# Which engine makes the low parts of the second MLP's down products: one of seven on VectorE, or four of seven

## What is computed

```python
        h2 = rmsnorm(x, mlp_norm_w[l])
        u = jax.nn.relu(jnp.einsum('bld,df->blf', h2, w_up[l]))
        x = x + jnp.einsum('blf,fd->bld', u * u, w_down[l])

    return rmsnorm(x, final_norm_w)
```

## Time and profile before

| | us |
|---|---|
| median of 3 runs | 1609.27 |
| lowest to highest | 1608.09 to 1610.73 |
| the profiled execution, by the same clock | 1609.46 |
| its span in the trace | 1607.6 |
| TensorE busy | 1563.9 (97% of the span) |
| VectorE busy | 916.2 (57%) |
| GpSimd busy | 790.2 (49%) |
| ScalarE busy | 531.6 (33%) |

### The profile page before, as it was taken

The page is one execution under the profiler, slowest core; times in us unless marked ns, Lnnn a source line. Parts: engine busy times, 40 slices in busy tenths (PEclk is TensorE's granted clock), DMA queues, the critical chain, the costliest instruction groups (busy, mean ns, idle before and its releaser), DMA issues.

```text
span 1607.6 us, 19248 instructions
## 1 busy us (share of the span) xinstructions
PE 1563.9 (97%) x7495; PEld 1286.0 (80%) x7495; DVE 916.2 (57%) x1185; ACT 531.6 (33%) x760; POOL 790.2 (49%) x289
## 2 busy tenths in 40 slices
PE   9999999999999999999999999999999998989886
PEld 7887788888888888888888887877789886868764
DVE  5902588900246666666006489987555156382798
ACT  3012121200135443443124244257433334242334
POOL 5874288677760445445440003421251448556476
PEclk9999999999999999999999999999999999999998
DMA  6232032233242332332232232221232503214021
GB/s 223 90 120 79 1 112 92 92 105 105 79 131 80 105 105 79 104 104 89 95 118 73 89 97 79 81 52 26 80 131 79 183 27 127 83 56 154 0 79 53
DMA packets 127382, 147.00 MB, mean 91 GB/s; under 512 B 5143, under 2 KB 98375, under 8 KB 127304
## 3 DMA queue, kind: packets, MB, share of 16 engines
q1 hardware_dynamic: 125430, 141.05, 27.9%
q10 hardware_dynamic: 1874, 4.85, 0.9%
HBM read 143.79 MB, written 2.10 MB: 91 GB/s over the span
## 4 chain that ended last, share of the span: by engine, by line
PE 85%; POOL 5%; DVE 4%; issue 3%; ACT 2%; DMA 1%; POOLq 0%; DVEq 0%; SPq 0%; ACTq 0%
PE ps L812 26%; PE ps L814 25%; PE ps L813 25%; PE ps L967 3%; PE ps L1042 2%; POOL w_lo L795 1%; POOL w_lo L797 1%; PE ps L1209 1%; POOL w_lo L759 1%; PE ps L1030 1%; POOL tail_lo L795 1%; PE ps L1226 1%; DVE a_lo L2290 1%; POOL w_hi L754 1%; DVE x L2237 1%
## 5 line engine op out<-in xcount | busy, mean ns | idle before, releaser
L759 POOL TENSOR_TENSOR w_lo<-raw,w_hi 128x1024 fp32r<-128x1024 f32 x166 | 420.5, 2554 | 496.4 <-ACT w_hi L1312 493.6
L812 PE MATMUL ps<-hT_hi,w_hi 128*128 128x512 f32 (+1 forms) x848 | 324.5, 383 | 0.8 <-POOL w_lo L759 0.5
L813 PE MATMUL ps<-hT_lo,w_hi 128*128 128x512 f32 (+1 forms) x848 | 323.2, 381 | 0.0
L814 PE MATMUL ps<-hT_hi,w_lo 128*128 128x512 f32 (+1 forms) x848 | 323.2, 381 | 0.0
L754 POOL TENSOR_TENSOR w_hi<-raw,cells 128x2048 fp32r<-128x2048 f32 x35 | 129.5, 3701 | 126.5 <-PE ps L812 125.3
L812 PEld LDWEIGHTS ps<-hT_hi,w_hi 128*128 128x128 f32 x848 | 159.4, 188 | 33.9 <-issue 2.3
L814 PEld LDWEIGHTS ps<-hT_hi,w_lo 128*128 128x128 f32 x848 | 159.4, 188 | 30.6
L813 PEld LDWEIGHTS ps<-hT_lo,w_hi 128*128 128x128 f32 x848 | 159.4, 188 | 30.4
L1312 ACT ACTIVATE w_hi<-raw 128x2048 fp32r<-128x2048 f32 (+1 forms) x58 | 109.6, 1890 | 128.3 <-PE ps L812 106.5
L812 PE MATMUL ps<-w_hi,hT_hi 128*128 128x512 f32 (+2 forms) x400 | 151.6, 379 | 0.0
L813 PE MATMUL ps<-w_lo,hT_hi 128*128 128x512 f32 (+2 forms) x400 | 150.1, 375 | 0.0
(11 more groups left out here) (368 smaller groups left out, 3161.7 us busy)
## 6 DMA issues: line engine op xcount, KB each, us to landing
raw<-in_w_in SPq DMA_DIRECT2D x86, 512.0 KB, 4.7
raw<-in_w_up SPq DMA_DIRECT2D x60, 512.0 KB, 4.8
raw<-in_w_down SPq DMA_DIRECT2D x34, 512.0 KB, 4.2
raw_tail<-in_w_down SPq DMA_DIRECT2D x20, 512.0 KB, 4.7
raw<-in_w_out SPq DMA_DIRECT2D x16, 512.0 KB, 4.2
raw_tail<-in_w_up SPq DMA_DIRECT2D x16, 512.0 KB, 4.9
raw<-in_w_ret_o SPq DMA_DIRECT2D x8, 512.0 KB, 4.0
raw<-in_w_sgu_o SPq DMA_DIRECT2D x8, 512.0 KB, 4.0
```

The costliest lines, as they stand in the source:

```text
L759: nc.gpsimd.tensor_tensor(lo[:, c], raw[:, s, c], hi[:, c].bitcast(f32), ALU.subtract).then_inc(unit_split, 1)
L812: first = nc.tensor.matmul(dst, a_hi, b_hi, start=start, stop=False, skip_group_check=onto)
L813: nc.tensor.matmul(dst, a_hi, b_lo, start=False, stop=False, skip_group_check=onto)
L814: return first, nc.tensor.matmul(dst, a_lo, b_hi, start=False, stop=stop, skip_group_check=onto)
```

## The change

Products 3, 5 and 6 of each set get their weights' low part from VectorE too, beside product 2; products 0, 1 and 4 and all ups stay with GpSimd. VectorE makes it right behind the `a_lo` of the same step. On ScalarE `a_hi` of a step now goes ahead of `hi` of the same step. TensorE's list and SyncE's list stay as they are. `AT` is only another name for the places in `STREAM`, and the rewritten conditions of the sums give the same sums in the same steps.

```diff
-VECTOR_LOW = 2
+VECTOR_LOW = (2, 3, 5, 6)
...
-    by_vector = [kind == "down" and n == VECTOR_LOW for kind, _, n in STREAM]
+    by_vector = [kind == "down" and n in VECTOR_LOW for kind, _, n in STREAM]
...
                 if at_v + 2 < N:
-                    tail_high(at_v + 2)
                     if STREAM[at_v + 2][0] == "down":
                         token_high(at_v + 2)
+                    tail_high(at_v + 2)
                 square(at_v, 0)
...
+                nearest = STREAM[at_v + 1]
+                if nearest[0] == "down" and 2 <= nearest[2] <= 4:
+                    weight_sum(nearest[1], ADDS[nearest[2] - 1])
                 if at_v + 2 < N and STREAM[at_v + 2][0] == "down":
                     token_low(at_v + 2)
+                    if low_count(at_v + 2)[0]:
+                        weight_low(at_v + 2)
...
-                if kind == "down" and n == 0:
-                    weight_low(at_v + 2)
                 take(at_v, 0)
```

More of the change, by code:

```diff
@@ L246 @@
 STREAM = second_mlp()
-START = [STREAM.index(("down", q, 0)) for q in range(FF2_Q)]
+AT = {step: v for v, step in enumerate(STREAM)}
 RAW_SLOTS, W_SLOTS, A_SLOTS = 5, 3, 3
 def low_count(v):
-    by_vector = [kind == "down" and n == VECTOR_LOW for kind, _, n in STREAM]
+    by_vector = [kind == "down" and n in VECTOR_LOW for kind, _, n in STREAM]
     return by_vector[v], by_vector[:v + 1].count(by_vector[v])
@@ L1675, in token_high @@
                 if a_n >= A_SLOTS:
-                    before = START[(a_n - A_SLOTS) // 7] + (a_n - A_SLOTS) % 7
+                    before = AT["down", (a_n - A_SLOTS) // 7, (a_n - A_SLOTS) % 7]
                     act.wait_ge(tail_started, before + 2)
@@ L2247, in weight_sum @@
                     await_loaded(dve, "down", q, "B12")
-                    await_low(dve, START[q])
+                    await_low(dve, AT["down", q, 0])
                     made = V.tensor_tensor(out, raw_part(q, "B12"), out, ALU.subtract)
@@ L2251, in weight_sum @@
                     await_loaded(dve, "down", q, "B22")
-                    await_low(dve, START[q] + 2)
+                    await_low(dve, AT["down", q, 2])
                     made = V.tensor_tensor(out, raw_part(q, "B22"), out, ALU.subtract)
@@ L2258, in weight_sum @@
                 else:
-                    await_low(dve, START[q] + 1)
+                    await_low(dve, AT["down", q, 1])
                     dve.wait_ge(weights_added, 4 * q + 2)
@@ L2303, in _ @@
                 kind, q, n = STREAM[at_v]
-                coming = next((c for c in range(FF2_Q) if START[c] - at_v in (1, 2)), None)
-                if kind == "down" and n == 0:
[L2306 to L2310, removed]
+                coming = next((c for c in range(FF2_Q) if AT["down", c, 0] - at_v in (1, 2)), None)
+                if kind == "down" and n < 2:
+                    token_sum(q, TOKEN_SUMS[2 + n])
                 if coming is not None:
-                    token_sum(coming, TOKEN_SUMS[2 - (START[coming] - at_v)])
+                    token_sum(coming, TOKEN_SUMS[2 - (AT["down", coming, 0] - at_v)])
+                nearest = STREAM[at_v + 1]
+                if nearest[0] == "down" and 2 <= nearest[2] <= 4:
+                    weight_sum(nearest[1], ADDS[nearest[2] - 1])
                 if at_v + 2 < N and STREAM[at_v + 2][0] == "down":
                     token_low(at_v + 2)
-                if coming is not None and START[coming] - at_v == 1:
+                    if low_count(at_v + 2)[0]:
+                        weight_low(at_v + 2)
+                if coming is not None and AT["down", coming, 0] - at_v == 1:
                     weight_sum(coming, "T1")
-                if kind == "down" and n == 0:
-                    weight_low(at_v + 2)
                 take(at_v, 0)
```

## The result

The changed kernel takes 1591.53 us (median of 4 runs, 1591.19 to 1593.82) against 1608.68 for the kernel before (1607.78 to 1610.73, 4 runs beside them): a ratio of 0.9895, with a 95% interval of 0.9878 to 0.9912, 17.2 us less. The forecast was 1593.5, in a range of 1580 to 1603.

What follows compares the result with a forecast made beforehand. Bound: a serial chain of GpSimd and VectorE instructions excluding each other on a shared port. Sets of 179.3 us plus 2.5 for the clock give 181.8 against 197.65, 15.9 less than 1609.27: forecast 1593.5 us, range 1580 to 1603.

Steps and rivals of the forecast that it cites:

- The bound: Second half of each set: GpSimd halves, T and `a_lo` exclude each other on a shared port, 8.0 us per product.
- Product 3: Its 4.45 us wait goes in sets 0 to 2; in set 3 it is 1.0 late, where it was 5.57.
- The new wait: Before product 4, for product 2's take queued behind standing T3 and `a_lo`: 2.9 us, in set 3 3.8.
- Products 5 and 6: VectorE's steps of 6.86 and 5.98 us against 5.44 make TensorE wait 1.4 and 0.5.
- Sets: The four sets take 43.0, 43.0, 48.4 and 44.9 us, 179.3 together, before the clock term.
- The clock: Slow matmuls behind five remaining waits, mostly swallowed by later waits: 2.5 us stay (0 to 9); clock in sets above 0.93.
- The 14 waits: Count of TensorE's waits in the sets after the change, against 11 before, each short; used in C and D.
- B: Takes don't bind: VectorE finds the port free, no stands at T3 and `a_lo`; 15.6 us over four sets, 1578; chance 0.14.
- C: Low clock is not swallowed and short waits pull it down too: 12.6 us instead of 2.5, 1603.5; chance 0.14.
- D: Slower: clock stays down through products 4 to 6 of each set, 1641 at the worst; chance 0.06.
- E: No effect: takes come later by as much as low parts come earlier; 1607 to 1611; chance 0.04.
- SyncE's loads: They wait for the same low parts, which come at the same time or earlier; effect 0.

Runs made afterwards that it cites:

- the run with the added matmuls: Changed kernel plus unused matmuls keeping TensorE busy: 13 behind product 3 of each set, 24 behind product 5 of set 2; 1591.28 us.
- the run with the early take: Changed kernel with one take moved: in product 5's step of set 2, VectorE takes the first half ahead of set 3's S3 and `a_lo`; 1591.39 us.

## Why the prediction was right

**The bound.** Right: GpSimd and VectorE in one serial chain. The run without product 4's low part shows it by taking one side away.

**Product 3.** Right: its wait is gone in all four sets, also in set 3, where 1.0 was to stay. The two runs with half of the change show that both parts of the working were needed.

**The new wait.** Forecast 2.9 before product 4 for the take; 2.80, 2.78 and 2.78 in sets 0 to 2, and 3.30 in set 3 for 3.8. T3 and the `a_lo` behind it were forecast at 3.8 and 3.4 and are 3.81 and 3.40.

**Products 5 and 6.** Forecast 1.4 and 0.5 behind VectorE steps of 6.86 and 5.98. In set 1 product 5 starts 6.87 after product 4 and product 6 6.11 after that. As waits they can be seen in set 1 alone (1.15 and 0.38); in sets 0, 2 and 3 slow matmuls stand where product 5's wait would be.

**Sets.** Forecast 43.0, 43.0, 48.4 and 44.9 without the clock; measured 43.23, 43.22, 49.93 and 43.89. Set 2 was 1.5 too short in the sum and set 3 1.0 too long: seven slow matmuls in product 6 of set 2 (it took 7.08 instead of 5.44) lengthened the one and gave VectorE the time that product 3 of set 3 was to wait for; with them taken away that wait was 0.93. The two together were forecast at 93.3 and took 93.8.

**The clock, the term that was mis-sized.** It was put at 2.5 us. Taking the slow matmuls away gave nothing that can be told from 0. The four sets are 1.0 above the sum without this term: half of it in sets 0 and 1, half in sets 2 and 3. The two misses pull against each other: the clock 2.5 too much, the rest 1.0 too little. So the sum of the sets lies 1.5 above what was measured, which is most of the 2.0 by which the forecast lies above the median. The argument (a low clock is swallowed by the next wait) was right and held for more than it was applied to. One sign was missed: the clock was to be above 0.93 in the sets, and in set 2 it is 0.93.

**The working.** Three counts in it are off, and none moves the forecast much. The "some 70" slow matmuls of the kernel before are some 60, 12.3 us behind six waits. The 14 waits to come are 13 by its own list. Take, `a_lo`, `w_lo` and two takes are 5.3, not 5.2.

**Rivals.** B, a free port: refuted by T3's 3.81. C and D, the clock gives the gain back: refuted by the run with the added matmuls; and the waits of 1.15 and 0.38 in set 1 had no slow matmul behind them, where C wanted short waits to pull the clock down. E, the takes come later by as much: refuted by steps of 6.87, where it needed those of the kernel before, 7.7 and more. SyncE's loads were put at nothing; no wait of TensorE names them in the changed kernel.

## What to carry to other kernels

Where two engines exclude each other, cost work by the time that the shared thing is held, and look at what is queued behind an instruction that will stand: here it was a take that freed an accumulator. Moving one more low part to the engine that is already late was faster (1585.6 for 1591.5), because it removed stands (3.8 us) longer than the work (2.2). With as many low parts on VectorE as in the changed kernel, but others of them, it was faster still (1583.3). A reordering and a move can each be worth little and much together, so a half that measures small is not yet refuted. And a wait that disappears is worth something only if the sum of its neighbours falls with it.

## What the runs showed of the hardware

The same wait of TensorE can cost a different amount of clock from one place to the next. In the changed kernel the wait before product 4 had slow matmuls behind it in sets 0, 2 and 3 (1.7 us each) and none in set 1, though the waits of sets 0, 1 and 2 are alike (2.80, 2.78 and 2.78). In the run with the early take, that wait (2.79) had some fourteen behind it in set 1.

VectorE's instruction with one input in the accumulators (the take of a product) does not stand for GpSimd: alone or beside one of GpSimd's halves it took 0.68 to 0.69, two in a row 1.40 to 1.42, in every run but for one pair of 1.52 in the run with the added matmuls.
